# Masking attention scores on VectorE in place in PSUM instead of by products with the identity on TensorE

## The reference, cut to what matters

```python
rel = s_idx - BLOCK - a_idx
mask = (jnp.abs(rel) <= WINDOW) & (key_pos >= 0) & (key_pos < L)
s_loc = jnp.einsum('bqkrd,bskd->bkrqs', qn, kn) * scale
s_loc = jnp.where(mask, s_loc, jnp.float32(-1e30))
s_ctx = jnp.einsum('bqkrd,bskd->bkrqs', qn, k_ctx) * scale
logits = jnp.concatenate([s_loc, s_ctx], axis=-1)
m = jnp.maximum(jnp.max(logits, axis=-1, keepdims=True), sink_l)
p = jnp.exp(logits - m)
denom = jnp.sum(p, axis=-1, keepdims=True) + jnp.exp(sink_l - m)
out = jnp.einsum('bkrqs,bskd->bqkrd', p / denom, vals)
```

## Time and profile before

| what | value |
|---|---|
| median of 3 runs | 2413.6 us (2408.51 to 2416.26) |
| the profiled execution | 2412.9 us, of which the span of the trace is 2411.1 us |
| TensorE busy | 2272.9 us (94%), 10924 instructions |
| VectorE busy | 935.4 us (39%) |
| ScalarE busy | 619.8 us (26%) |
| mean granted TensorE clock | 0.979 |
| read from HBM | 568.97 MB |

### The profile page before, as it was taken

The page is one execution under the profiler, slowest core; times in us unless marked ns, Lnnn a source line. Parts: engine busy times, 40 slices in busy tenths (PEclk is TensorE's granted clock), DMA queues, the critical chain, the costliest instruction groups (busy, mean ns, idle before and its releaser), DMA issues.

```text
span 2411.1 us, 25343 instructions
## 1 busy us (share of the span) xinstructions
PE 2272.9 (94%) x10924; PEld 1483.0 (62%) x10924; DVE 935.4 (39%) x1265; ACT 619.8 (26%) x874; POOL 143.4 (6%) x138
## 2 busy tenths in 40 slices
PE   7999999999999999999999997999898989898998
PEld 5865878877888888886678884434343434343433
DVE  4847545458788334686623423000000000000001
ACT  5315233243334235336533211000000000000001
POOL 0122000210000011220000110000000000000000
PEclk9999999999999999999999998999999999999999
DMA  7220443435554341320012228999999999999997
GB/s 303 99 82 9 172 158 143 154 109 215 199 186 164 140 140 70 114 71 1 1 58 82 105 105 333 428 428 428 427 428 429 427 428 427 427 428 427 428 426 302
DMA packets 70606, 572.69 MB, mean 238 GB/s; under 512 B 5424, under 2 KB 5552, under 8 KB 38752
## 3 DMA queue, kind: packets, MB, share of 16 engines
q1 hardware_dynamic: 65936, 524.56, 53.1%
q0 software_dynamic: 3264, 29.49, 3.3%
q10 hardware_dynamic: 1296, 17.04, 1.9%
HBM read 568.97 MB, written 2.10 MB: 237 GB/s over the span
## 4 chain that ended last, share of the span: by engine, by line
PE 36%; DMA 17%; DVE 3%; ACT 1%; issue 1%; SPq 0%; DVEq 0%; ACTq 0%
PE ps L1311 10%; PE ps L791 9%; DMA arena<-in_w_exp_up 8%; PE ps L1411 6%; DMA arena<-in_w_exp_gate 4%; DMA weights<-in_w_exp_gate 3%; PE ps L1290 3%; DVE arena L2103 1%; PE ps L1186 1%; PE ps L1166 1%; DMA weights<-in_w_exp_up 1%; PE ps L1331 1%; DMA weights<-in_w_exp_down 1%; PE ps L1124 1%; PE ps L1143 1%
## 5 line engine op out<-in xcount | busy, mean ns | idle before, releaser
L791 PE MATMUL ps<-weights_r 128*128 128x512 f32 (+1 forms) x2784 | 856.8, 388 | 14.4 <-DVE hT_r L2009 7.3
L791 PEld LDWEIGHTS ps<-weights_r 128*128 128x128 f32 x2784 | 521.9, 189 | 127.7 <-issue 15.2
L791 PE MATMUL ps<-hT_r,weights_r 128*128 128x512 f32 x1264 | 462.8, 390 | 0.0
L1311 PE MATMUL ps<-weights,arena 128*64 128x512 f32 x768 | 352.5, 616 | 54.9 <-DMA weights<-in_w_exp_up 44.1
L1313 PE MATMUL ps<-weights,arena 128*64 128x512 f32 x768 | 353.2, 617 | 0.0
L1311 PEld LDWEIGHTS ps<-weights,arena 128*64 128x64 f32 x768 | 105.6, 141 | 281.4 <-issue 280.0
L1990 DVE TENSOR_TENSOR weights_r<-weights,weights_r 128x4096 fp32r<-128x4096 f32 (+1 forms) x45 | 192.7, 4281 | 213.1 <-ACT weights_r L1502 211.4
L791 PEld LDWEIGHTS ps<-hT_r,weights_r 128*128 128x128 f32 x1264 | 238.4, 189 | 49.6 <-issue 0.5
L791 PE MATMUL ps<-arena_r,weights_r 128*128 128x512 f32 (+1 forms) x640 | 225.2, 388 | 0.0
L1502 ACT ACTIVATE weights_r<-weights 128x4096 fp32r<-128x4096 f32 (+1 forms) x46 | 161.6, 3512 | 193.0 <-PE ps L791 115.6
L2628 DVE TENSOR_TENSOR hT<-hT,ps 128x512 f32<-128x512 f32 x32 | 22.0, 688 | 454.9 <-PE ps L1313 454.9
(11 more groups left out here) (317 smaller groups left out, 2417.7 us busy)
## 6 DMA issues: line engine op xcount, KB each, us to landing
weights<-in_w_exp_gate SPq DMA_DIRECT2D x48, 2048.0 KB, 23.0
weights<-in_w_exp_down SPq DMA_DIRECT2D x42, 2048.0 KB, 27.1
weights<-in_w_exp_up SPq DMA_DIRECT2D x42, 2048.0 KB, 27.1
weights<-in_w_in SPq DMA_DIRECT2D x18, 2048.0 KB, 7.8
arena<-in_w_exp_gate SPq DMA_DIRECT2D x16, 2048.0 KB, 26.8
arena<-in_w_exp_down SPq DMA_DIRECT2D x14, 2048.0 KB, 27.1
arena<-in_w_exp_up SPq DMA_DIRECT2D x14, 2048.0 KB, 28.8
weights<-in_w_up SPq DMA_DIRECT2D x11, 2048.0 KB, 8.1
```

The lines of the kernel that those rows point to most:

```text
L791: last = pe.matmul(t, a if w_first else b, b if w_first else a, start=(k == 0 and n == 0), stop=(k == kt - 1 and n == len(pairs) - 1))
L1311: la = pe.matmul(bank(b0 + n)[0:64, :], xe[:, 2 * j + r, 0:64], wa[:, r, n * 512:(n + 1) * 512], start=start, stop=stop)
```

## The change

The two rounded copies and the mask products are gone, and the local products close their own accumulation. `att_max` adds the mask, straight from the constants in SBUF, to the neighbour blocks of both heads in PSUM by one `tensor_tensor` before the reduction, and waits for it by `link`.

```diff
-        mask_r = at(18048, 2, P, rounded=True)
-        ident_r = at(17920, P, rounded=True)
+        mask = const("mask").rearrange("p (m s) -> p m s", m=2)
...
                     local = pe.matmul(ps[:, c:c + w], q2[o:o + 64, 2 * kv + p, n * P:(n + 1) * P],
-                                      kdup[o:o + 64, kv, b0 * P:b1 * P], start=True, stop=False)
+                                      kdup[o:o + 64, kv, b0 * P:b1 * P], start=True, stop=True)
                 local.then_inc(S["as_half"], 1)
-                for o, c in heads:
-                    if len(masked(n)) == 2:
-                        t = ps[:, c:c + w].rearrange("p (b s) -> p b s", s=P)[:, 0:3:2, :]
-                        pe.matmul(t, ident_r, mask_r, start=False, stop=True)
-                    else:
-                        (b, m), = masked(n)
-                        pe.matmul(ps[:, c + b * P:c + b * P + P], ident_r, mask_r[:, m, :],
-                                  start=False, stop=True)
...
-            pe.wait_ge(S["mask_ready"], 2)
...
-            A(ident_r, ident, ACT.Copy).then_inc(S["mask_ready"], 1)
-            A(mask_r, const("mask").rearrange("p (m s) -> p m s", m=2), ACT.Copy).then_inc(S["mask_ready"], 1)
...
             def att_max(i, p):
-                kv, _, _, _, nb = window(i)
+                kv, n, _, _, nb = window(i)
                 c, h = 3 * 512 * p, 4 * kv + 2 * p
                 ve.wait_ge(S["as_full"], 4 * i + 2 * p + 2)
+                blocks, ms = slice(masked(n)[0][0], masked(n)[-1][0] + 1, 2), slice(masked(n)[0][1], masked(n)[-1][1] + 1)
+                t = ps[:, c:c + 2 * nb * P].rearrange("p (g b s) -> p g b s", g=2, s=P)[:, :, blocks, :]
+                link(ve.tensor_tensor(t, t, wide(mask[:, ms, :].unsqueeze(1), P, 2, len(masked(n)), P), ALU.add))
                 link(ve.tensor_reduce(tops[:, p, :],
```

More of the change, by code:

```diff
@@ L323, in build_two_blocks @@
             merged_ready conv_mid gelu_ready act_ready ln_ready ln_stats ln_root ya_ready exp_done
-            kdup_ready mask_ready as_half as_full nm_ready sink_arg sink_exp at_full at_kept_a at_kept_d
+            kdup_ready as_half as_full nm_ready sink_arg sink_exp at_full at_kept_a at_kept_d
             r_ready pv_full pv_free row_ready aff_exp router_in router_w aff_ready rank_ready sel_ready wsel_full
```

## The result

The changed kernel took 2396.4 us (median of 6 runs, 2390.0 to 2404.3) against 2413.2 us (6 runs) before: a ratio of 0.9936, with a 95% interval of 0.992 to 0.9952. A second series gave 2396.3 us (5 runs) against 2415.1 (15 runs), 0.9924 (0.9911 to 0.9936). The gain is 17 to 19 us, or 0.6 to 0.8%. The forecast was 2402, a gain of 10.7 us, with a range that ended at 2398. The direction held, and so did the account of what hides the additions; the size did not, because one step in TensorE's account was wrong.

A forecast was written before the change was run, and what follows sets the result against it. TensorE was taken to bound the attention stretch (busy 152.1 of 160 us). 13.0 - 0.3 (fit) - 0.9 (start) - 0.5 (end) - 0.6 (`as_half`) = 10.7 us, so 2412.9 becomes 2402, range 2398 to 2409.

The forecast's parts named there:

- The products left stay as they are: TensorE in the attention loop: local and context products keep their times, so only the mask products' 13.0 us leave.
- What TensorE loses: TensorE in the attention loop: 32 mask products leave, in slots of 0.44 and 0.37 us per half, 13.0 us in all.
- The additions' price: VectorE's 32 additions in PSUM: 0.73 us (five blocks) and 0.46 us (four) with the link, together 19.0 us.
- the end's 0.46: Loop's end: the last exponential follows one more addition and delays the first gate product, 0.46 us lost.
- The rival of a dearer write: VectorE's addition into PSUM costs up to 1.22 and 0.69 us; some 5 us lost, 2407; chance 0.17.
- a pause inherited by the context products: Rival on TensorE: the row change's 7.5 us stay, only 5.4 us leave, giving 2410; chance 0.10.
- The fit: Additions hide in VectorE's 2.00 us wait for transpose 3, using it up; only one round is late, by 0.3 us.
- The start: Loop's start: new 0.55 us TensorE wait at the scores of (2, 1), plus some 0.3 for a late copy; 0.9 us.
- `as_half`: Signal of a half's second local product: TensorE's waiting product loses 0.04 us each, 0.6 in all, at most 2.7.
- The pass-on through the experts: Experts behind the loop: transfers start when TensorE frees buffers, so the loop's gain passes on one to one.
- the cases within 0.3%: Whole kernel's change within 0.3% (7.2 us): half the dear addition, the inherited pause and the swallowing experts; chance 0.23.
- the slower case: Rival: VectorE becomes the bound, additions over 1.3 us; at 1.8 us, 2425; chance 0.05, in the sum 0.06.

The follow-up runs named there:

- no_mask: The changed kernel without VectorE's mask addition, so neither engine masks and the output isn't the reference's: loop 122.23 us against 123.91, whole 2394.5 us.
- add_twice: The changed kernel with VectorE's mask addition made twice, each with its wait: loop 134.68 us against 123.9, whole 2409.1 us (1 run).
- recip_later: The changed kernel with VectorE's reciprocal of the denominators moved behind the first maximum: loop 123.86 us against 123.91, whole 2399.6 us.
- exp_first: recip_later, with ScalarE in iteration 1 making the exponentials of (1, 0) ahead of its copy of transpose 2: loop 122.92 us, whole 2400.2 us (1 run).
- mask_rows64: The kernel before with mask products on 64 rows, half the queries unmasked, `as_half` raised by the last: loop 125.55 us against 137.90, whole 2396.5 us (1 run).
- mask_fp32: The kernel before with its mask products in fp32 on all 128 rows, two passes each: loop 152.31 us against 137.90, whole 2421.5 us (1 run).
- both: The kernel before with VectorE's additions on top of the mask products: loop 138.39 us, 0.49 more than before; whole 2411.9 us, ratio 0.9989.
- combo: exp_first, with the first gate product waiting for 63 exponentials instead of 64: loop 122.54 us, whole 2397.2 us, ratio 0.9931.
- combo2: combo, with VectorE in iteration 1 taking the maximum of (1, 1) ahead of its copy of transpose 3: loop 121.12 us, whole 2395.6 us, ratio 0.9913.

## Why the prediction was wrong in size, by its own steps

- **"The products left stay as they are"** (What TensorE loses) is the step that failed. The mask products' slot was read rightly as 13.0 us, and it did leave. But the 64-row products of the two heads overlap among themselves, and a product on all 128 rows beside them takes a part of that overlap away: 0.09 us ahead of it, and up to 0.10 behind it. By no_mask TensorE's part is 15.7 us over the loop, at a pace of 4.28 instead of 3.24 us per four iterations, which over 16 units would be 17.1; the difference of 1.4 is near the 1.5 that iteration 2 loses at the low clock. The forecast said outright that the context products would start 0.84 and 0.63 us behind the local ones; they start at 0.75 and 0.54. The 7.5 us above streaming were seen and named as the change from 64 to 128 rows, but I looked for its price only between the starts of the mask and context products, and not inside its neighbours. The Trainium skill (TensorE: Matmul & The Clock Gate, Part 3, The mechanism) says that weight loads overlap with products in flight only where their row groups differ. The two experiments on the rows agree with that: 1.18 us with 64-row masks, 1.90 with 128-row ones. The formula of the Trainium skill (TensorE: Matmul & The Clock Gate, Back-to-back issue gap), which I weighed against the rows, gave an estimate of 6.1 us; the price of the barrier isn't in it.
- **The additions' price** (0.73 and 0.46) was right: 0.67 to 0.70 and 0.41 to 0.43 measured, and the end's 0.46 came out as 0.48 (changed kernel against no_mask). The rival of a dearer write falls, as does that of a pause inherited by the context products.
- **The fit** was right as a mechanism: add_twice shows the cover used up and the named wait. The size in the middle was 0.8 us, where I had 0.3. TensorE arrives some 0.16 us a round sooner than I had counted (two halves at 0.52 instead of 0.44), which goes that way, but the place was wrong too: the one round that I had called late, into iteration 10, lost 0.13 with the iteration behind it, and iterations 6 and 7 lost 0.40. Why those was not found. That the sink's wait was a part of it was refuted by recip_later.
- **The start** was priced at 0.9 us and cost 0.4, but for another reason: the clock fell behind the 1.80 us wait and slowed TensorE, which hid VectorE's lateness. With the clock kept up (exp_first) the foreseen wait appears: 1.68 us, of which 1.17 are TensorE's earlier arrival, so 0.51 where I had 0.55. The wait's price was right, and that it didn't cost more in the changed kernel was luck.
- **`as_half`** was priced at 0.6 us and cost nothing. The changed kernel shows no pause there: the five-block context products take 0.65 us (0.64 before). No run tests why the estimated delay doesn't show.
- **The pass-on through the experts** was right: the shift reaches the end. What it didn't hold is the rest: 2411.1 - 2392.2 = 18.9 us of span, of which 14.0 are the loop, 1.4 the way to the router, explained by the clock, 1.5 the start ahead of the loop, which moves between 1068.3 and 1074.6 in these kernels without order, and 2.0 the stretch of the experts. Why the last differs was not found: from the router on, the kernel before takes 957.5 and 957.7 us in its two traces, the changed one 955.5 and 955.4. It doesn't go with the masks: recip_later, mask_rows64 and mask_fp32 take 955.1 to 955.5, and no_mask, both, exp_first, combo, combo2 and add_twice 957.1 to 957.6.

With TensorE's part at 15.7 (13.0 forecast) and losses of 1.7 (2.3 forecast), the sum would have been 14.0 for the loop. By the loop alone the time would have been 2412.9 - 14.0 = 2398.9, just inside the range of 2398 to 2409. The medians say 16.8 and 18.8, and it is the surplus that took the time out of the range. Of the 6.1 us between a gain of 10.7 and one of 16.8, 2.7 are TensorE's part, 0.6 the losses, and 2.8 lie outside the loop. In the two first traces what lies outside is the start ahead of the loop, the fall of the clock and the experts; in the other kernels none of them goes with the masks, so this part is chance, as far as is known, and no step of the forecast. Two of the forecast's own figures don't add up: the chances of the cases within 0.3% come to 0.245 where the text has 0.23, and the slower case has 0.05 and 0.06.

## What to carry to other kernels

Where products on half of the rows run one behind another for two heads, products on all rows among them cost more than their own slot (15.7 us here for a slot of 13.0): cost them by removing them, or by what their neighbours take elsewhere without them, and not by the gap between starts. A cheap operation moved onto a half-idle engine is hidden only as far as that engine's longest round of waits has idle time: measure that round, and treat it as spent afterwards. A stretch that repeats within hundredths of a microsecond in the trace tells variants apart that whole runs can't.

## What the runs showed that I had not expected

- The clock fell to 0.50 for some 3 us behind a 1.80 us wait of TensorE in four kernels without 128-row masks (changed, no_mask, recip_later, mask_rows64), and didn't behind the same wait in those with them (before, both, mask_fp32). But it didn't fall in add_twice either, which has the wait and no such masks. Where the wait was cut to 0.63 us it didn't fall; behind the later wait of 1.68 us in exp_first it stayed at 1.00 too. So neither the wait nor the masks alone decide it, and what does is left open.
- The fall of the clock between 1408 and 1432 us, in a stretch where TensorE is busy throughout, repeats for a kernel but differs between kernels whose code is the same there: 0 to 3.4 us of missing clock. A change elsewhere of a few microseconds can so win or lose as much again, without a cause of its own.
- VectorE adds in place in PSUM at the price of an addition that only reads from there: 0.41 to 0.43 us for 256 columns and 0.67 to 0.70 for 512, where the kernel before has 0.42 and 0.69 on the mean.
